# Six gate chunks move from the recurrence's filling to its input stage, as Strassen pairs, and the last two stages of layer 1 are joined

## What is computed

```python
u = rms_norm(x, p['norm_g']) * (1.0 + scale[:, None]) + shift[:, None]
proj = u @ p['w_in']
q_a, kv_a, k_rope, z_mla, cb, cc, cx, z_conv, rw, z_rw, g_merge = split_cols(proj)
...            # attention -> y_mla, short convolution -> y_conv
rw_s, shift_state = token_shift(rw, shift_prev, p['rwkv_mu'])
...            # S = S*w + sa(x)(kk*a) + v(x)k, y = S r, one step per token -> y_rw
gm = jax.nn.sigmoid(g_merge)
merged = (gm[..., :D_MODEL] * y_mla + gm[..., D_MODEL:2 * D_MODEL] * y_conv
          + gm[..., 2 * D_MODEL:] * y_rw)
x = x + gate[:, None] * (merged @ p['w_out'])
```

## Time and profile before

| | us |
|---|---|
| median of 3 runs (3476.80 to 3479.68) | 3477.43 |
| the profiled execution, its own time | 3476.93 |
| its span, first to last instruction | 3475.1 |
| PE busy with products | 3332.8 |
| DVE / ACT busy | 1761.7 / 947.5 |

### The profile page before, as it was taken

How to read it: one execution, slowest core, us unless ns; L and a number is a source line. 1 busy time by engine, 2 the same in 40 slices (tenths; PEclk the granted TensorE clock), 3 DMA queues, 4 the chain that set the end, 5 groups by cost and what they waited for, 6 DMA issues and landing times. The chain is left out here.

```text
span 3475.1 us, 66271 instructions
## 1 busy us (share of the span) xinstructions
PE 3332.8 (96%) x28751; PEld 2242.8 (65%) x28751; DVE 1761.7 (51%) x3347; ACT 947.5 (27%) x2040; POOL 147.6 (4%) x175
## 2 busy tenths in 40 slices
PE   7999999999999999999989999999999999999997
PEld 5876655666566677765668866566665666776665
DVE  5543055454446788644355611545453567885522
ACT  3101023233255422211121011233232553222201
POOL 1000000000000022100000000000000001220000
PEclk8999999999999999999999999999999999999999
DMA  7112111121220377486021121111213105774521
GB/s 249 31 52 58 37 59 49 55 59 51 68 56 16 124 274 274 178 279 234 13 76 42 46 58 48 49 53 51 59 53 77 39 10 196 275 274 163 182 83 58
DMA packets 250919, 357.03 MB, mean 103 GB/s; under 512 B 47395, under 2 KB 222301, under 8 KB 242054
## 3 DMA queue, kind: packets, MB, share of 16 engines
q1 hardware_dynamic: 217590, 180.49, 17.3%
q0 software_dynamic: 16400, 155.53, 12.2%
q10 hardware_dynamic: 16640, 16.78, 1.5%
HBM read 302.17 MB, written 48.35 MB: 101 GB/s over the span
## 5 line engine op out<-in xcount | busy, mean ns | idle before, releaser
L1286 PE MATMUL rwkv_gate_bank<-u,stream_ring 128*128 128x364 f32 (+1 forms) x2304 | 788.3, 483 | 2.0 <-PEq L1197 2.0
L1286 PEld LDWEIGHTS rwkv_gate_bank<-u,stream_ring 128*128 128x128 f32 x2304 | 413.3, 190 | 219.2 <-issue 8.8
L606 PE MATMUL rwp_b<-u,stream_ring 128*128 128x364 f32 (+1 forms) x864 | 265.0, 468 | 7.2 <-PEq L1035 7.2
L2663 PE MATMUL dec_s_bank<-u,att_q_rows 32*64 32x256 f32 x8192 | 243.6, 384 | 0.0
L606 PEld LDWEIGHTS rwp_b<-u,stream_ring 128*128 128x128 f32 x864 | 163.5, 190 | 105.4 <-issue 8.0
L3050 PE MATMUL out_b<-merged,w_out 128*128 128x364 f32 (+1 forms) x672 | 214.5, 471 | 3.6 <-PEq L2926 3.6
L2663 PEld LDWEIGHTS dec_s_bank<-u,att_q_rows 32*64 32x64 f32 x8192 | 188.9, 134 | 36.2 <-issue 11.7
L3050 PEld LDWEIGHTS out_b<-merged,w_out 128*128 128x128 f32 x672 | 128.3, 191 | 81.7 <-issue 5.8
L2719 ACT ACTIVATE page_probs<-dec_s_bank,dec_minus_top 128x1024 f32<-128x1024 f32 x64 | 71.3, 1114 | 336.1 <-DVE dec_minus_top L2756 336.1
L2326 PE MATMUL attn_s<-u 96*128 96x512 f32 (+3 forms) x384 | 148.4, 496 | 3.7 <-ACT attn_probs L2400 3.7
L1300 ACT ACTIVATE rwkv_gate_stage<-rwkv_gate_bank 128x364 f32<-128x364 f32 x144 | 67.6, 470 | 294.7 <-PE rwkv_gate_bank L1286 294.2
(11 more groups left out here) (616 smaller groups left out, 5381.1 us busy)
## 6 DMA issues: line engine op xcount, KB each, us to landing
stream_ring<-in_w_in_dram SPq DMA_DIRECT2D x98, 512.0 KB, 4.1
merge_sig<-gates_feature_major SPq DMA_DIRECT2D x16, 1632.0 KB, 9.6
gates_feature_major<-rwkv_gate_stage SPq DMA_DIRECT2D x96, 182.0 KB, 1.9
u<-in_w_ada_dram ACTq DMA_DIRECT2D x16, 1024.0 KB, 13.7
gates_feature_major<-rwkv_gate_stage SPq DMA_DIRECT2D x48, 180.0 KB, 2.0
w_out<-in_w_out_dram SPq DMA_DIRECT2D x14, 512.0 KB, 11.1
start_ada<-in_w_ada_dram SPq DMA_DIRECT2D x6, 1024.0 KB, 11.5
x_feature_major<-o_mla SPq DMA_DIRECT2D x2, 2176.0 KB, 7.5
```

The lines of the kernel that those rows point to most:

```text
L606: mm = pe.matmul(self.banks[j % len(self.banks)][:, 0:m], self.stream.w(c, k), s.u[:, k, t0:t0 + m], start=(k == 0), stop=(k == KD - 1))
L1286: mm = pe.matmul(self.banks[j % 2][:, 0:m], self.stream.w(self.first + n, k), self.s.u[:, k, t0:t0 + m], start=(k == 0), stop=(k == KD - 1))
L2663: mm = pe.matmul(S[64 * half:64 * half + NQ, 512 * i:512 * i + NK], q, keys, start=(cb == 0), stop=(cb == BLOCKS))
```

## The change

Three things are done in both layers and one in layer 1 alone.

1. `project_rwkv` takes the first six gate chunks and the first six `rw` chunks as six pairs (12 passes); three chunks stay plain. `u_sums` is kept alive for it, and the pairs' home is `s.o_side`, which still holds `s.o_conv`: SP's store of it becomes the first DMA of the stage and DVE waits for its landing before the first weight sum. The gate results are written to the end of `raw_p`, from where SP stores them; before each further gate pair, and before the first `rw` pair, DVE waits until the stores have landed.
2. The filling has 18 chunks, 432 products. `fill(23)` becomes `fill(12)`, and `fill(3)` after `inv_t` becomes `fill(2)`: 49 filling products a block.
3. Buffers of the recurrence are allocated from the other side of the memory, so that they can coexist with `u_sums`; three small tiles are laid into `rows`.
4. In layer 1 `output_and_final_norm` does both stages: groups of 384, 384 and 320 tokens, four banks in place of five, the tiles of a finished group transposed between the products of the next, the last three tiles at the end; stores go by SP.

```diff
--- before
+++ after
...
-    NW, LONE = 2, 3
+    NW, LONE, EARLY_GATES = 2, 3, 6
...
-            for stage, chunks in (("mla", self.mla(l)), ("conv", self.w_in(l, COL_CB, 8)), ("rwp", self.w_in(l, COL_RW, 9)),
-                                  ("gates", self.w_in(l, COL_GM, 3 * KD)), ("attn", self.attention(l)), ("merge", self.merge(l))):
+            for stage, chunks in (("mla", self.mla(l)), ("conv", self.w_in(l, COL_CB, 8)), ("rwp", self.w_in(l, COL_GM, self.EARLY_GATES) + self.w_in(l, COL_RW, 9)),
+                                  ("gates", self.w_in(l, COL_GM + P * self.EARLY_GATES, 3 * KD - self.EARLY_GATES)), ("attn", self.attention(l)), ("merge", self.merge(l))):
...
-        self.n, self.stream, self.first = n_chunks, s.stream, s.stream.first[stage, l]
+    def __init__(self, ph, s, stage, l, n_chunks, n_banks, skipped=0):
+        self.n, self.stream, self.first = n_chunks, s.stream, s.stream.first[stage, l] + skipped
...
-def project_rwkv(nc, s, l, raw_p, raw_s, load_next):
-
-    N_CHUNKS = 9
+def project_rwkv(nc, s, l, u_sums, raw_p, raw_s, rows, load_next):
+
+    N_GATES = s.stream.EARLY_GATES
+    GATE_PASSES, N_PASSES, N_CHUNKS = N_GATES, N_GATES + 6, N_GATES + 9
     R = SHIFT_W // P
     with Phase(nc, "rwp") as ph:
-        pr = Projection(ph, s, "rwp", l, N_CHUNKS, 6)
-        rows = ph.sb("rows", [BATCHES, SHIFT_W])
-        out_s = ph.sb("out_s", [BATCHES, SHIFT_W])
-        out_p = ph.sb("out_p", [R, P])
+        pair = PairProjection(ph, s, u_sums, "rwp", l, tuple(range(0, N_PASSES, 2)), [ph.bank(f"p{i}") for i in range(3)],
+                              s.o_side[:].rearrange("p k t -> p (k t)"))
+        pr = Projection(ph, s, "rwp", l, N_CHUNKS - N_PASSES, 3, skipped=N_PASSES)
...
+        gate_words = raw_p[:].rearrange("p k t -> p (k t)")[:, R * (1 + SEQ) - 2 * T:]
+        gate_pieces = [gate_words[:, x * T:(x + 1) * T].rearrange("p (k h t) -> p k h t", k=2, h=2) for x in range(2)]
...
+        def out(i, k, t0):
+            if i < GATE_PASSES:
+                return [(gate_pieces[i % 2][:, k, t0 // HALF_T], lambda a: a)]
...
+                def store_gates(i):
+                    sp.wait_ge(pair.added, 8 * (i + 1))
+                    for k in range(2):
+                        columns = s.gates_dram[i // 2 * 2 + k].rearrange("p (h x t) -> p h x t", h=2, x=2)[:, :, i % 2]
+                        sp.dma_start(columns, gate_pieces[i % 2][:, k]).then_inc(gate_stored[i % 2], 16)
+
+                sp.dma_start(s.o_side_dram[0:2].rearrange("k p n -> p k n"), s.o_conv).then_inc(conv_out, 16)
+                sp.dma_start(past, s.ins["state_rwkv_shift"][l]).then_inc(state_in, 16)
...
+                for p in range(N_PASSES // 2):
+                    if 2 * p < GATE_PASSES:
+                        store_gates(2 * p)
+                    pair.load_behind(sp, p)
+                    if 2 * p < GATE_PASSES:
+                        store_gates(2 * p + 1)
+                for n in range(pr.n - 1):
...
-                for n in range(N_CHUNKS):
+                for i in range(N_PASSES):
+                    pair.products(pe, i)
...
+                    pair.keep_both(act, i)
...
+                def both_passes(p):
+                    pair.even_pass(dve, 2 * p, out)
+                    if 2 * p + 2 < N_PASSES:
+                        pair.odd_pass(dve, 2 * p + 1, out)
+                    else:
+                        pair.even_pass(dve, 2 * p + 1, out)
+
+                dve.wait_ge(conv_out, 16)
+                for j in range(5):
+                    pair.sum_weights(dve, 0, j)
+                for p in range(N_PASSES // 2):
+                    if 0 < p < GATE_PASSES // 2:
+                        for x in range(2):
+                            dve.wait_ge(gate_stored[x], 32 * p)
+                    if p == GATE_PASSES // 2:
+                        for x in range(2):
+                            dve.wait_ge(gate_stored[x], 16 * GATE_PASSES)
+                        dve_s.done(dve.memset(raw_p[:, :, 0:1], 0.0), "zeros")
+                    both_passes(p)
...
-        self.jobs = [(n, g) for n in range(3 * KD) for g in range(NG)]
+        self.early = s.stream.EARLY_GATES
+        self.jobs = [(n, g) for n in range(self.early, 3 * KD) for g in range(NG)]
...
-                    fill(23)
+                    fill(12)
...
-                        fill(3)
+                        fill(2)
...
+        project_rwkv(nc, s, l, u_sums, raw_p, raw_s, rows, load_recurrence)
+        free_sums()
...
+def output_and_final_norm(nc, s, l, merged, w_out):
+
+    NB, GROUPS = 4, ((0, 384), (384, 384), (768, 320))
+    jobs = [(g, n) for g in range(len(GROUPS)) for n in range(KD)]
...
+                for i in range(n_tiles):
+                    t0, n = tokens(i)
+                    sp.wait_ge(scaled, i + 1)
+                    dst = s.outs["y_prompt"][0, t0:t0 + n, :] if i < SEQ // P else s.outs["y_sample"].rearrange("b t d -> (b t) d")
+                    sp.dma_start(dst, row[0:n, i % 2, :]).then_inc(stored[i % 2], 16)
...
+                def turn(i):
                     t0, n = tokens(i)
                     if i >= 2:
                         pe.wait_ge(scaled, i - 1)
                     for k in range(KD):
-                        mm = pe.transpose(B[i % 2][0:n, k * P:(k + 1) * P], residual(s, k)[:, t0:t0 + n], s.tab["ident"])
+                        if i >= tiles_of(last)[0] and k in (0, KD - 1):
+                            pe.wait_ge(added, KD * last + (KD if k else KD - 1))
+                        mm = pe.transpose(rows_of[i % 2][0:n, k * P:(k + 1) * P], residual(s, k)[:, t0:t0 + n], s.tab["ident"])
                     mm.then_inc(turned, 1)
+
+                for j, (g, n) in enumerate(jobs):
+                    t0, m = GROUPS[g]
+                    if j >= NB:
+                        pe.wait_ge(added, j - NB + 1)
+                    for k in range(KD):
+                        mm = pe.matmul(banks[j % NB][:, 0:m], w_out[k][:, n * P:(n + 1) * P], merged[:, k, t0:t0 + m],
+                                       start=(k == 0), stop=(k == KD - 1))
+                    mm.then_inc(multiplied, 1)
+                    if g and n in (1, 3, 5):
+                        if n == 1:
+                            pe.wait_ge(added, KD * g)
+                        turn(tiles_of(g - 1)[n // 2])
+                for i in tiles_of(last):
+                    turn(i)
...
+                    if g and n in (2, 4, 6):
+                        scale(tiles_of(g - 1)[n // 2 - 1])
+                for i in tiles_of(last):
+                    scale(i)
...
+                if l + 1 < DEPTH:
+                    output_projection(nc, s, l, merged, w_out)
+                else:
+                    output_and_final_norm(nc, s, l, merged, w_out)
```

More of the change, by code:

```diff
@@ L1215, in _ @@
+                for n in range(pr.n):
                     pr.multiply(pe, s, n)
                     if n == 0:
-                        pe.wait_ge(state_in, 16)
-                        for k in range(R):
-                            mm = pe.transpose(turn[:, 8 * k:8 * k + 8], rows[:, k * P:(k + 1) * P], s.tab["ident"][0:8, 0:8])
-                        pe_s.done(mm, "state")
-                    if n == R - 1:
-                        pe.wait_ge(pr.emptied, NG * 4)
+                        pe.wait_ge(pair.added, 8 * N_PASSES)
@@ L3052, in _ @@
                     mm.then_inc(multiplied, 1)
-                    if more and n == 1 and j > KD:
+                    if n == 1 and j > KD:
                         sums(j // KD - 1)
-                if more:
-                    sums(2)
+                sums(2)
             @block.vector
@@ new lines, in _ @@
+                root(2)
+                shift(2)
+def output_and_final_norm(nc, s, l, merged, w_out):
+    NB, GROUPS = 4, ((0, 384), (384, 384), (768, 320))
+    jobs = [(g, n) for g in range(len(GROUPS)) for n in range(KD)]
+    tokens = lambda i: (i * P, P) if i < SEQ // P else (SEQ, SAMPLE)
+    n_tiles, last = SEQ // P + 1, len(GROUPS) - 1
+    tiles_of = lambda g: [i for i in range(n_tiles) if GROUPS[g][0] <= tokens(i)[0] < sum(GROUPS[g])]
+    prompt_of = lambda g: min(GROUPS[g][1], SEQ - GROUPS[g][0])
+    with Phase(nc, "out") as ph:
+        tmp = ph.sb("tmp", [P, SAMPLE])
+        sq = ph.sb("sq", [P, D_MODEL])
@@ L3158, in final_norm @@
         row = ph.sb("row", [P, 2, D_MODEL])
[L3159 to L3160 removed]
+        final_g = ph.sb("final_g", [P, D_MODEL])
+        ms = ph.sb("ms", [P, n_tiles])
         eps = ph.sb("eps", [P, 1])
[L3162 to L3164 removed]
+        banks = [ph.bank(f"b{i}") for i in range(NB)]
@@ L3165, in final_norm @@
+        rows_of = [ph.bank(f"rows{i}", (P, D_MODEL)) for i in range(2)]
+        x_in = [ph.sem(f"x_in{g}") for g in range(len(GROUPS))]
+        multiplied, added, gated, g_in = (ph.sem(n) for n in ("multiplied", "added", "gated", "g_in"))
```

(3 more changed lines are left out.)

219 lines of the change are left out of this document (113 added, 106 removed).

## The result

The changed kernel takes 3458.8 us (median of four runs, 3457.6 to 3460.5) where the one before took 3478.6 beside it (3476.8 to 3480.9). The medians are 19.7 us or 0.57% apart; the ratio on record, with its 95% interval, is 0.9938 (0.9923 to 0.9952), or 0.62% less. The profiled execution took 3459.1, 1.9 more than its span.

The account below looks back on a forecast made before the run. PE's products were taken to bound the kernel; -43.0 + 3.8 + 8.5 + 1.2 + 15.3 - 5.0 = -19.2 gave span 3455.9 and time 3458.2 us. Its own range was 3450 to 3466, the full range 3442 to 3471.

Parts of the forecast that it names:

- pairs for plain chunks: Input stage and filling: per layer twelve chunks at 14.62 leave, twelve passes at 12.83 come; -43.0 us for both layers.
- start of the input stage: PE waits 1.3 to 2.9 us, taken as 1.9, for a weight sum behind the convolution store; +3.8 both layers.
- filling at m = 32 and m = 8: Removed merge products given back: +8.5 us at m = 32 before `u_0`, +1.2 at m = 8 of block 0.
- end of the recurrence: 16 products a layer move here, mostly passing time while DVE's chain sets the end; +15.3 us, bounds nothing and 19.5.
- joined last stages: Layer 1's end: 24.3 us in place of 29.9, half-clock transposes allowed for; -5.0, bounds -2 and -7.
- Rival 4: Input-stage pairs slower than the convolution's as DVE awaits gate stores, or half the merges give back; +12 to +20, chance 0.07.
- Filling, 23 to 12: At a block's start twelve products just cover DVE's `kh`; zero cost, some 0.5 us slack, up to 1 per block otherwise.
- blocks 0 to 6: Where m = 32 gives its removed product back as waiting for `inv_x`: 14 x 0.61, +8.5 us over both layers.
- Rival 3: Filling of two does not cover the merges; the other four give back too, 39 us, 3497; chance 0.07.
- Rival 2: Clock falls after waits at input stage's start and recurrence's end; 6.8 to 13.6 us more, 3465 to 3472; chance 0.16.
- the 3 products ahead, 1.8, and the 0.27: 2.1: Recurrence's end: only products ahead of the last state update and DVE's pause for PE shorten the chain, 2.1 us a layer.
- rival 1: Covers hold: chains at m = 32 and the recurrence's end move up with PE; -44 us, 3433; chance 0.08.

Follow-up runs that it names:

- the give-back alone: Kernel before the change with only fill(23) made fill(12) and the merges' fill(3) made fill(2), all 24 chunks still in the filling: 3483.0 us, ratio 1.0010.
- the fastest kernel: Changed kernel with fill(2) for fill(4) ahead of merges, third product back at m = 32 in blocks 0 to 6, none around block 7's state updates: 3434.5 us.
- filling kept for the end: Changed kernel with fill(2) in place of fill(4) ahead of the merges, 16 products a layer left for the recurrence's end: 3441.5 us, ratio 0.9895.

## Why the prediction was right, and where it was not

The time came out 0.6 us from the forecast, but the terms did not. By terms, both layers, from the stage table and the runs above (the table of profiles adds up to -17.9, where the forecast's terms give -19.2):

| term | predicted | measured | from |
|---|---|---|---|
| pairs for plain chunks | -43.0 | -43.0 | passes at 12.83, no gaps |
| start of the input stage | +3.8 | +5.2 | 69.24 and 68.48 longer, less 66.24 for twelve passes against six chunks |
| filling at m = 32 and m = 8 | +9.7 | +9.1 | the give-back alone: 4.6 and 4.5 |
| end of the recurrence | +15.3 | +19.3 | what is left: 175.4 removed, 147.0 gone from the stages, less 9.1 |
| joined last stages | -5.0 | -12.6 | stage table, and alone |
| others | 0 | +4.1 | below |

**Pairs.** Right, with DVE's waits for gate stores hidden as argued. Rival 4, slower pairs, is out with it.

**Filling, 23 to 12, and in the merges.** Right in kind and size. A block is 9.12 us shorter (predicted 9.2). In block 1 of the changed kernel the merges m = 8 to 32 start 0.36 to 0.39 after the inverse that they wait for, as predicted, and the gap at `u_0` is 0.74 in blocks 1 to 6 where I had "0.6 to 0.8". Too broad was "blocks 0 to 6": block 0 had a gap of 1.11 there already and kept it, and block 1's grew by 0.27 alone. And the sum for twelve products at a block's start leaves 0.2 of slack (609.2 less 609.04), not the "0.5" that stands there. Rival 3, all merges giving back, is out: the kernel with the two numbers changed would have been 39 us slower.

**Start of the input stage.** The mechanism was right and the size low. The wait stands bare, at full clock, in two starts: 2.04 in layer 1 of the fastest kernel, where the store lands in 5.2, and 2.71 with the last stages apart, where it lands in 5.9. Both are inside the bounds of 1.3 to 2.9; the step took 1.9 from a landing near the quiet 4.3. The loads behind the store do stretch it: in the twelve starts with the store ahead the landing was 5.2 nine times and 5.9 to 6.5 three times. The rest of the +5.2 is layer 0, where two groups at half clock take 3.1 us more than at full clock and so outlast the wait.

Rival 2 was in part true, since in 12 of the 14 starts in profiles of kernels with pairs a stretch of half clock stands here. But with the store ahead it was not the wait that brought it: the kernel with the joined last stages alone, which has no wait there, has it too after the same 3.60 of idle time, for 6.8 us, and its stage takes 137.52 in place of 134.46. The Trainium skill, TensorE: Matmul & The Clock Gate, Loop structure matters more than you think, has a long wait for DMA between matmuls turn PE cold. The traces agree for the wait of 4.3 with the store behind the loads, after which the granted clock was 0.51. They do not for the wait of 2.71 with the last stages apart, over which the clock stayed at 1.00. In the changed kernel the 6.8 that rival 2 put on the start was not paid in addition to the wait.

**End of the recurrence.** The step that failed is "what moves the chain is the 3 products ahead, 1.8, and the 0.27: 2.1". From the last `u_0` to attention the time went from 25.98 to 25.39 in layer 0 and from 26.17 to 26.52 in layer 1: 0.6 and -0.35, not 2.1. The 1.8 for the three products ahead came back in both layers: DVE's last state follows the `u_0` after 7.23 in place of 9.03. What took it away again is the clock. It falls in the 4.59 idle before `mean`, and from `mean` to DVE's copy of the last state it is 5.55 us (931.27 to 936.82) in place of 4.34 (936.59 to 940.93); in layer 1 it is 5.95 in place of 4.34. With filling kept for the end, where PE is busy there, the clock stays. In layer 1 another 0.67 is lost behind the chain, where attention starts 7.71 after the issue of the samples' states in place of 7.04. The prediction also has the states' landing end the stage; it is the gate store behind them, as shown above. I had named the fall of the clock at this place as a rival and priced it only behind the stage, not inside the chain. So nearly the upper bound of 19.5 was given back, and rival 1, in which this chain moves up with PE, is out.

**Joined last stages.** The mechanism was right, the term mis-sized. "Four times (0.62 - 0.17) each, 1.8 a tile" took a tile for sixteen records; a transpose is one record and eight of them take 0.87, so six tiles cost 5.2 and not 10.8. And the tail from the last product's end (3445.3) to the end of the span is 11.9, not 13.5: tile 6 takes 4.3, tile 8 4.0, and the store 3.5 where I had 4.5. 29.9 - 11.9 - 5.2 = 12.8, measured 12.6.

**What the sum owes to luck.** The joined stages brought 7.6 more than I said, and the start, the end and the other stages took 9 back. Of these the 4.1 of the others is mostly one stage that the change does not touch: the decoding of layer 0 took 305.9 in this profile and 300.5 before. It is not chance alone. In the three profiles without pairs this stage takes 300.5 to 300.7, in the seven with pairs 301.5 to 305.9, and in all seven PE stands idle for 0.8 to 1.4 us some 122 us into it, waiting for nothing that the profile shows. In layer 1 only one profile has something like it (302.3). What it comes from stays open.

## What to carry to other kernels

When work that fills waits is made cheaper or moved away, ask of each place whether the filling there was longer than the wait; what is over belongs where the filling runs out, and here dealing it out anew was worth some 24 us on top of the 20 us of the change itself. Count an engine's idle time at a place also for what it does to the clock of the work behind it, inside the chain that ends last. Before a row is multiplied, see how many records one operation leaves in it.

## What the runs showed of the hardware

**The clock falls while PE is busy.** In the samples' part of the recurrence, with products of 64x8, the granted clock falls with no idle time over 0.22 in the 18 us ahead of it. In layer 1 of the fastest kernel a stretch of 13.7 us runs at half clock, which layer 0 does not have; the same 64 products take 3.59 and 2.04 us (timeline, then window, layer 1 ahead of layer 0):

```profile
2237.51 3.59 PE L1510 MATMUL rwkv_t<-rwkv_kr,rw_state_s 64*64 64x8 f32 x64
```

```profile
2233.00:2247.00 14.00, 14.00 (x130) 9.27 (x128) 10.21 (x20) 0.00 (x0) 0.00 (x0) 0.51 0.01 2
```

```profile
541.16 2.04 PE L1510 MATMUL rwkv_t<-rwkv_kr,rw_state_s 64*64 64x8 f32 x64
```

```profile
538.00:552.00 14.00, 11.87 (x162) 7.45 (x158) 12.27 (x23) 1.30 (x2) 0.00 (x0) 1.00 0.00 1
```

It makes the stage 5 to 6 us longer (432.90 against 427.03; 445.43 against 439.25 with the store behind the loads), came in one layer each of four profiles of ten, and in neither layer of the other six. Shorter stretches are the rule there: 19 of the 20 recurrences have at least 3.4 us of half clock between 33 and 58 us from their start, the kernels before and after too. It may be a part of why the runs of a kernel spread by some 10 us here; that is argued, not shown.

**The clock after the same idle time is not always the same.** After 3.59 or 3.60 us of idle time the input stage began at full clock in both layers of the kernel before, and in 3 of the 18 other starts; in 15 there were about 3.4 or 6.8 us of half clock at or near the start.

**SP's issue of a transfer takes longer when much is under way:** the first load of `rw_wa` took 3.50 us to issue in the changed kernel, with the big store ahead of it, and 1.40 with the store behind the loads (layer 0 of both).
